# One upright inverse per level, turned over by VectorE: block 2's triangular inverses in a two-block forward pass

## The reference

```
def step(state, inp):
    r_t, w_t, k_t, v_t, kk_t, b_t = inp
    sk = einsum('bhvk,bhk->bhv', state, kk_t)
    state = state * w_t - sk[..., None] * b_t + v_t[..., None] * k_t
    return state, einsum('bhvk,bhk->bhv', state, r_t)
```

## Time and profile before

| | before |
|---|---|
| median of 3 runs | 1098.51 us (1097.63 to 1099.61) |
| the profiled execution: its own time | 1098.23 us |
| the profiled execution: its span | 1096.4 us |
| PE busy, PEld busy | 1085.6 us (99%), 929.3 us (85%) |
| DVE, ACT, POOL busy | 702.8, 233.1, 147.8 us |
| mean of the DMA queues over the span | 149 GB/s |

### The profile page before, as it was taken

The page is one execution under the profiler, slowest core; times in us unless marked ns, Lnnn a source line. Parts: engine busy times, 40 slices in busy tenths (PEclk is TensorE's granted clock), DMA queues, the critical chain, the costliest instruction groups (busy, mean ns, idle before and its releaser), DMA issues.

```text
span 1096.4 us, 22053 instructions
## 1 busy us (share of the span) xinstructions
PE 1085.6 (99%) x9150; PEld 929.3 (85%) x9150; DVE 702.8 (64%) x1600; ACT 233.1 (21%) x610; POOL 147.8 (13%) x204
## 2 busy tenths in 40 slices
PE   9999999999999999999999999999999999999997
PEld 8899899999988599999546888888888888887883
DVE  4376674766743477777657677666766667666465
ACT  4131221313200111010002331322223132324101
POOL 1100000000045221100330012020120202020042
PEclk9999999999999999999999999999999999999999
DMA  8677657553366446564562432333232332161251
GB/s 294 235 274 256 191 176 229 178 173 97 116 212 229 153 80 232 194 214 155 185 256 97 135 85 91 102 98 111 78 108 87 98 96 61 41 231 40 79 152 38
DMA packets 62773, 163.26 MB, mean 149 GB/s; under 512 B 8625, under 2 KB 22865, under 8 KB 62674
## 3 DMA queue, kind: packets, MB, share of 16 engines
q1 hardware_dynamic: 61666, 160.22, 45.3%
q10 hardware_dynamic: 1008, 1.63, 0.4%
HBM read 160.73 MB, written 1.11 MB: 148 GB/s over the span
## 4 chain that ended last, share of the span: by engine, by line
PE 94%; DVE 5%; DMA 1%; issue 0%; ACT 0%; POOL 0%; DVEq 0%; ACTq 0%; POOLq 0%
PE bank L813 21%; PE bank L966 20%; PE bank L465 19%; PE bank L879 6%; DVE arena L2357 3%; PE bank L1123 3%; PE bank L625 3%; PE bank L745 2%; PE bank L788 2%; PE bank L1279 2%; PE bank L1110 2%; PE bank L941 1%; PE bank L1001 1%; PE bank L541 1%; PE bank L947 1%; PE bank L979 1%
## 5 line engine op out<-in xcount | busy, mean ns | idle before, releaser
L966 PE MATMUL bank<-hT,slots 128*128 128x256 f32 x1120 | 254.6, 382 | 0.0
L966 PEld LDWEIGHTS bank<-hT,slots 128*128 128x128 f32 x1120 | 209.8, 190 | 28.4
L465 PE MATMUL bank<-hT,slots 128*128 128x256 f32 x544 | 119.7, 379 | 0.0
L465 PEld LDWEIGHTS bank<-hT,slots 128*128 128x128 f32 x544 | 103.0, 190 | 14.4 <-issue 0.6
L2357 DVE SCALAR_TENSOR_TENSOR arena<-padA,par,arena 128x256 f32<-128x256 f32 x232 | 114.1, 556 | 0.0
L465 PE MATMUL bank<-arena,slots 128*128 128x256 f32 x432 | 94.2, 379 | 0.7 <-DMA slots<-in_w_br 0.7
L465 PEld LDWEIGHTS bank<-arena,slots 128*128 128x128 f32 x432 | 81.9, 190 | 12.2 <-DMA slots<-in_w_br 1.1
L813 PE MATMUL bank<-hT,slots 128*128 128x128 f32 x736 | 91.7, 276 | 0.0
L813 PEld LDWEIGHTS bank<-hT,slots 128*128 128x128 f32 x736 | 86.7, 192 | 0.7 <-issue 0.7
L2787 POOL TENSOR_TENSOR arena<-arena 128x256 f32<-128x256 f32 x40 | 33.2, 853 | 358.7 <-PE bank L941 297.1
L813 PE MATMUL bank<-arena,slots 128*128 128x128 f32 x640 | 79.6, 275 | 0.0
(11 more groups left out here) (433 smaller groups left out, 1701.1 us busy)
## 6 DMA issues: line engine op xcount, KB each, us to landing
slots<-in_w_rwkv SPq DMA_DIRECT2D x72, 512.0 KB, 3.6
slots<-in_w_heads SPq DMA_DIRECT2D x68, 512.0 KB, 4.6
slots<-in_w_gu SPq DMA_DIRECT2D x44, 512.0 KB, 4.5
arena<-in_ada_w SPq DMA_DIRECT2D x24, 512.0 KB, 5.3
slots<-in_w_down SPq DMA_DIRECT2D x20, 512.0 KB, 4.0
slots<-in_w_br SPq DMA_DIRECT2D x32, 256.0 KB, 2.7
slots<-in_w_out SPq DMA_DIRECT2D x16, 512.0 KB, 4.2
slots<-in_w_y SPq DMA_DIRECT2D x16, 512.0 KB, 5.8
```

What stands on the lines that cost most here:

```text
L465: end = e.matmul(psum, w[:, k * P:(k + 1) * P], rhs[:, k, :], start=k == 0, stop=k == kt - 1)
L966: end = e.matmul(proj(w, q), slot[w][:, k * P:(k + 1) * P], hT[:, k, :], start=k == 0, stop=k == KT - 1)
```

## The change

- PE's step N1 (8 products for each pair) goes.
- In `inverted(l)` for l = 1 to 4, PE makes Zs by Gs with all 64 columns, and no longer Gs by Zs: 8 products of 64 columns take the place of 16 of 32. At l = 5 it stays with 8 of 32.
- ScalarE copies the new half of the columns out of bank 3 as before, with the stride now on the side of PSUM.
- VectorE's copy of Zs (l = 1 to 4) is replaced by a transpose of Xs into Zs, in squares of 32 (up to l = 4 the inverses are made of diagonal blocks of at most 32). It now waits for ScalarE's copy where the copy waited for PE.
- VectorE's two operations for the first Xs are replaced by a transpose of the first Zs, which waits for GpSimd. GpSimd makes the first Zs ahead of Nm1.
- Two moves: at l = 1 and l = 3 the masking of M and RBK goes ahead of the transpose on VectorE; for j = 0 the tanh of the gate goes behind the copy of N and tokV on ScalarE.
- `grown(l)` on PE waits for the same steps as before (X of ScalarE, Z of VectorE, Nm of GpSimd).

```diff
@@ pe_rwkv, inverted(l)
                 e.wait_ge(*dve.upto(f"G{l}.{j}"))
-                for b, lhs, rhs, half_of in ((3, Z, Gs, 0), (2, Gs, Z, 1)):
-                    if l < LEVELS - 1 or half_of:
-                        for c in range(CHUNKS):
-                            for r in HEAD_ROWS:
-                                end = e.matmul(bank[b][r, c * HD // 2:(c + 1) * HD // 2].rearrange("p (n s) -> p n s", s=size),
-                                               lhs[r, c, :], columns_of(rhs[r, c, :], half_of, size), start=True, stop=True)
+                for c in range(CHUNKS):
+                    for r in HEAD_ROWS:
+                        if l < LEVELS - 1:
+                            end = e.matmul(chunks(half(3))[r, c, :], Z[r, c, :], Gs[r, c, :], start=True, stop=True)
+                        else:
+                            end = e.matmul(bank[2][r, c * HD // 2:(c + 1) * HD // 2].rearrange("p (n s) -> p n s", s=size),
+                                           Gs[r, c, :], columns_of(Z[r, c, :], 1, size), start=True, stop=True)
                 end.then_inc(*pe.step(f"XZ{l}.{j}"))
@@ pe_rwkv
                 to_tokens(e, chunks(bank[2][:, T:]), vT, cst2_of("centre")).then_inc(*pe.step(f"N.{j}"))
-                products(e, chunks(half(3)), A, B).then_inc(*pe.step(f"N1.{j}"))
@@ act_rwkv
-                e.activation(all_columns_of(Xs, 0, 2 ** l), joined(3, 2 ** l), ACT.Copy).then_inc(*act.step(f"X{l}.{j}"))
+                e.activation(all_columns_of(Xs, 0, 2 ** l), columns_of(half(3), 0, 2 ** l), ACT.Copy).then_inc(*act.step(f"X{l}.{j}"))
             if j == 0:
                 act_value(e, 1)
-                act_gate(e, 1)
...
                 e.activation(tokV[j % 2], chunks(bank[2][:, T:]), ACT.Copy).then_inc(*act.step(f"tokV.{j}"))
+            if j == 0:
+                act_gate(e, 1)
@@ dve_rwkv
+            def turned(l):
+
+                e.wait_ge(*(act.upto(f"X{l}.{j}") if l else pool.upto(f"Z0.{j}")))
+                to, of, name = (Zs[j % 2], Xs, "Z") if l else (Xs, Zs[j % 2], "X")
+                e.transpose(flat(to), flat(of)).then_inc(*dve.step(f"{name}{l}.{j}"))
...
-            if levels:
-                e.wait_ge(*pe.upto(f"N1.{j}"))
-                e.tensor_tensor(Xs, chunks(half(3)), each(cst2_of("off_first")), ALU.mult).then_inc(*dve.step(f"X0.m.{j}"))
             if chain:
                 solved(0)
             if levels:
-                e.wait_ge(*dve.upto(f"X0.m.{j}"))
-                e.tensor_tensor(Xs, Xs, each(cst2_of("unit")), ALU.add).then_inc(*dve.step(f"X0.{j}"))
                 e.wait_ge(*pe.upto(f"bonus.{j}"))
                 e.tensor_tensor(bonus[j % 3], vT, half(5), ALU.mult).then_inc(*dve.step(f"bonus.{j}"))
-                taps(e, j, *((14, 18) if not j else (18, 27) if more else (18, 22)))
+                taps(e, j, *((14, 16) if not j else (18, 21) if more else (18, 20)))
+                turned(0)
+                taps(e, j, *((16, 18) if not j else (21, 27) if more else (20, 22)))
...
-                inverted(1)
                 e.wait_ge(*pe.upto(f"M.{j}"))
                 e.tensor_tensor(Mt[j % 2], chunks(bank[6][:, T:]), each(cst2_of("st")), ALU.mult).then_inc(*dve.step(f"M.{j}"))
+                turned(1)
...
-                inverted(2)
+                turned(2)
...
-                inverted(3)
                 e.wait_ge(*pe.upto(f"RBK.{j}"))
                 e.tensor_tensor(RBK[j % 2], chunks(bank[5][:, :]), each(cst2_of("up"), 2 * CHUNKS), ALU.mult).then_inc(*dve.step(f"RBK.{j}"))
+                turned(3)
...
-                inverted(4)
+                turned(4)
@@ pool_rwkv
-            blocks(1)
             e.tensor_tensor(Zs[j % 2], Nt, each(cst2_of("off")), ALU.mult).then_inc(*pool.step(f"Z0.m.{j}"))
             e.wait_ge(*pool.upto(f"Z0.m.{j}"))
             e.tensor_tensor(Zs[j % 2], Zs[j % 2], each(cst2_of("unit")), ALU.add).then_inc(*pool.step(f"Z0.{j}"))
+            blocks(1)
```

More of the change, by code:

```diff
@@ L458, in joined, with flat @@
             return bank[b][:, 0:P].rearrange("p (n s) -> p n s", s=size)
+        def flat(tile):
+            return tile.rearrange("p c n -> p (c n)")
         HEAD_ROWS = (slice(0, HD), slice(HD, P))
```

## The result

| | before | after |
|---|---|---|
| median, runs of the comparison | 1098.88 us (1097.63 to 1099.61) | 1081.7 us (1080.96 to 1082.11) |
| ratio, with its 95% interval | | 0.9844 (0.9827 to 0.9861) |
| profiled execution: span | 1096.4 us | 1079.7 us |
| stage of the eight pairs | 370.87 us | 353.90 us |

The change makes the kernel 17.2 us faster, 1.6%. The forecast was 20.5 us less work and 0.3 for small delays (1078.0 us), in a range of 1074.8 to 1087: the time lies 3.7 us above the forecast. It is the better measure between single profiles: the stage starts anywhere between 623.6 and 625.1 us in the profiles of this study, though nothing ahead of it differs. By it the change gives 16.97 us.

The account below looks back on a forecast made before the run. PE, 99% busy, bounds the kernel, except ahead of `forced(1)` in the middle pairs, where VectorE does. 18.6 + 0.47 + 1.2 + 0.2 = 20.5 us less gives 1077.7, with 0.3 for delays 1078.0 us; range 1074.8 to 1087.

Parts of the forecast that it names:

- the two regimes: Ahead of `forced(1)` in the six middle pairs VectorE sets the time; elsewhere PE does.
- PE's products of a level: Levels 1 to 4, eight pairs: a group falls from 1.05 to 0.47 us, 0.58 less each, 18.6 us in all.
- The bound I put beside it: Levels 1 to 4: new products as slow per half as the old make a group 0.53, the sum 1.7 us smaller.
- the signs under which I had called the prediction wrong: Transposes of 0.6 or more, PE waiting at `inverted(3)` or `inverted(5)`, or new groups over 0.53.
- N1: Start of each pair, PE step removed: 0.47 us gained in the first, 1.2 in six middle pairs, 0.2 in the last.
- The transpose's price: On VectorE, 128x256: taken as 0.42 us, between 0.29 and 1.75; among the taps 0.42 to 0.67.
- rivals 1 and 2: Transpose dearer, 0.6 to 1.3 us: 1085.2 us, chance 0.17; VectorE becomes the bound through it: 1104.8 us, chance 0.07.
- The waits at levels 1 to 4: VectorE's transpose waiting for ScalarE's copy of Xs: idle time behind it covers the delay, PE loses nothing at 0.42.
- GpSimd's order and the moved tanh: Ahead of the first transpose and in the first pair: hidden by PE's fill and a 1.84 us wait, cost nothing.
- The page against the row: Levels 1 to 4: by the skill page a level saves 0.33 us, 10.7 in all, near 1086; the sum used the row.
- the 0.3 us for delays: Added to the forecast time for small semaphore delays that the added link may bring.
- my own case: Transpose up to 0.6 us: from 23.8 us less, 1074.4, to 16.8 less, 1081.4; chance 0.72.

Follow-up runs that it names:

- experiment 5: The changed kernel with two of the nine VectorE taps ahead of `forced(1)` moved to the end of the call before; 1077.3 us, ratio 0.9796.
- split_group: The changed kernel with one fill product of 128x256 moved from behind each XZ group at levels 1 to 4 into its middle; 1093.98 us, ratio 0.9950.

## Why the prediction was right, and what in it was off

- **What bounds the kernel, and the two regimes**: right. PE's work taken out came out of the time wherever PE set it; ahead of `forced(1)` in the middle pairs VectorE did, as the chain of waits had shown, and experiment 5 shows it by removing it.
- **PE's products of a level**, 0.58 us x 32 = 18.6: the term that was mis-sized. It measured 0.44, 14.0 in all. The step that failed is "33 ns each" against "29 ns each": I divided a group with costly edges (L1123 starts behind a wait and is followed by L928's products of 128x128) and compared it with one amid its like (N1, between other products of 64x64), so the new group was given no edge and the old one's edge was counted as its products' price. The bound I put beside it (0.53 for the new group) missed as well; it measured 0.57 to 0.62, which is one of the signs under which I had called the prediction wrong. The rows that would have told were in the same trace, a group of 32 halves (level 2) and one of 16 (level 5) of the kernel before, both between the same kinds of neighbours, 1.00 and 0.53 us, which leaves 0.47 for 16 halves:

```profile
732.60 1.07 PE L1123 MATMUL bank<-arena 64*64 64x32 f32 x32
733.60 0.71 PE L933 MATMUL bank<-arena 128*128 128x128 f32 x4
...
757.83 0.61 PE L1123 MATMUL bank<-arena 64*64 64x32 f32 x16
758.36 0.92 PE L966 MATMUL bank<-hT,slots 128*128 128x256 f32 x3
```

- **N1**: 1.9 us forecast, 2.90 measured by itself. Middle pairs 0.31 instead of 0.2 (the bonus starts 0.66 earlier where I had 0.75, since I had taken 716.99 from the chain, where a piece begins when the one before it ends, and VectorE's timeline has it at 716.91; and the transpose, not slowed among the taps, takes 0.35 of it), the first pair 0.48 (0.47 forecast), the last 0.63 instead of 0.2: there PE's 0.47 came through and 0.16 of short waits at `forced(1)` and `inverted(1)` went with it.
- **The transpose's price**: right (the 0.42 was a guess between 0.29 and 1.75, and it was a good one), 0.44 for 0.42, and so rivals 1 and 2 fell; they needed 0.6 and 1.38.
- **The waits at levels 1 to 4**: nothing was lost at any, as forecast. At level 2, the tightest, the count had `shift` 0.37 + 0.42 = 0.79 late against 0.63 and 0.24 of idle time, which leaves 0.08. It came 0.76 late and used up the 0.63, but the work up to the copy of `forced(2)` took 0.12 less than before, and so all of the 0.24 ahead of `grown(3)` is still there:

```profile
730.70 0.45 DVE L2427 STREAM_TRANSPOSE arena<-arena 128x256 f32<-128x256 f32 x1 [2.78 <-ACT arena L1609]
...
734.67 0.22 DVE L2403 COPY arena<-bank 128x64 f32<-128x64 f32 x1
735.12 0.42 DVE L2421 TENSOR_TENSOR arena<-bank,arena 128x256 f32<-128x256 f32 x1 [0.23 <-PE bank L1113]
```

- **GpSimd's order and the moved tanh**: free, as forecast; the first pair keeps all of PE's 0.47.
- **The page against the row.** By the Trainium skill, "TensorE: Matmul & The Clock Gate", section "Wait — 56ns, not 53.3ns?", a level would have saved 0.33 us, by my reading of the row 0.58, and it saved 0.44. The Trainium skill's 29 ns at 64 columns is what the runs show on average, but its 25 ns at 32 columns is not: these halves take 29.2 there too, in twos that start 7 ns apart. The row I set against it was right about the group and wrong about the product.
- **The sum**: 20.5 - 4.6 (levels) + 1.0 (N1) = 16.9, and 16.97 was measured in the stage. The two errors have opposite signs, and the 0.3 us for delays didn't show.
- **The range, and luck in it**: my own case ended at 16.8 us less, 1081.4 us, with a transpose of 0.6 and 33 ns for every half. Neither held, and still the result only came to this edge: 1081.7 us, 17.0 us less in the stage. The range took it in because it was drawn wide for rival 1, the dear transpose, which fell.

What sets the 29.2 ns of a half isn't settled: each one has a weight load of 64x64 and a product in the trace, they go in twos, and no run separated these.

## What to carry to other kernels

Price a group of small matmuls by the difference between two groups of different length on the same footing, not by dividing one group: for products of 64x64, taken in turn for two heads, each half costs 29 ns whether it has 32 columns or 64, and a change between 64x64 and 128x128 weights costs a third of a microsecond there and back. So drop whole products rather than columns, and keep small products in one run.

Where PE is 99% busy, follow the chain of waits through one period all the same: a wait of 0.2 us that repeats can stand for a stretch that another engine sets, and there a cut in PE's work comes through only as far as that engine gives way. Idle time ahead of each waiting operation, summed along an engine, told here which added work would be free and where the rest would be paid; its sizes were up to 0.24 us too high at a place in a middle pair, and it missed most of what the last pair lost.

## What the runs showed of the hardware that was not expected

- Products of 64x64 with 32 and with 64 columns cost the same, 29.2 ns on average for each of a float32 product's two rows, which start in twos, 7 ns apart, every 58 ns; halving the columns saved 0.03 us a group, once.
- Passing from products of 128x128 weights to products of 64x64 and back: 0.34 us each time in the middle pairs (split_group, 11.44 us for 32 in all), paid on both sides. Whether the array's shape or the size of the weights is the reason wasn't separated.
- VectorE's transpose of 128x256 in float32 takes 0.43 to 0.45 us, and 0.35 from its start to the next operation, with GpSimd at work, while the taps around it go from 0.41 to 0.71 us each on average (2.13 for three; single ones start 0.87 apart). The Trainium skill, "SBUF — State Buffer", section "Who interferes with whom", says that a VectorE instruction with at most one SBUF input, outside the two-port modes, doesn't contend with GpSimd, and that one with two does with a GpSimd instruction that reads SBUF. The transpose has one, a tap has two, GpSimd's maskings read SBUF, and the rows agree.
- The time at which the stage begins, after some 624 us of unchanged work, scatters by 1.5 us between profiled executions, more than some of the effects sought; lengths of the stage agree within 0.1 us with the sums of parts.
